# A hybrid decoder block on one core: outputs of the recurrence transposed by VectorE blocks and DMAs instead of TensorE

## The reference

```
def step(state, inp):
    q_n, k_n, u_n, w_n, qk_n, gc_n = inp
    v_new = u_n - einsum('bhcd,bhde->bhce', w_n, state)
    o = (einsum('bhcd,bhde->bhce', q_n * exp(gc_n)[..., None], state)
         + einsum('bhcs,bhse->bhce', qk_n, v_new))
    ...
    return state, o
...
o_a = o_a * rsqrt(mean(o_a * o_a, axis=-1, keepdims=True) + EPS)
o_a = o_a * gdn_norm_w * silu(gz)
y = sigmoid(mga) * (o_a @ w_branch_a) + sigmoid(mgb) * (o_b @ w_branch_b)
```

## Time and profile before

| | |
|---|---|
| median of 3 runs | 1130.29 us (1129.98 to 1130.35) |
| profiled execution | 1130.06 us |
| its span, first to last instruction | 1128.2 us |
| TensorE busy | 1118.4 us (99%) |
| ScalarE, VectorE, GpSimd busy | 456.5, 518.8, 538.7 us (40, 46, 48%) |
| recurrence, four chunks | about 163 to 400 us |

### The profile page before, as it was taken

How to read it: one execution, slowest core, us unless ns; L and a number is a source line. 1 busy time by engine, 2 the same in 40 slices (tenths; PEclk the granted TensorE clock), 3 DMA queues, 4 the chain that set the end, 5 groups by cost and what they waited for, 6 DMA issues and landing times.

```text
span 1128.2 us, 16308 instructions
## 1 busy us (share of the span) xinstructions
PE 1118.4 (99%) x5879; PEld 940.8 (83%) x5879; DVE 518.8 (46%) x1128; ACT 456.5 (40%) x759; POOL 538.7 (48%) x332
## 2 busy tenths in 40 slices
PE   9999999999999999999999999999999999999997
PEld 8788888888888888888888888888888888888885
DVE  5666456464646357777777562241222222220004
ACT  6465443435343365555555333423222222221122
POOL 5345674443524265555555544903444444444443
PEclk9999999999999999999999999999999999999999
DMA  7333333231313254444444375502333333222331
GB/s 212 80 91 95 101 105 103 66 103 57 94 48 112 71 155 118 123 123 128 122 120 121 105 246 147 188 26 75 93 93 93 96 106 95 93 94 94 100 105 75
DMA packets 169139, 120.45 MB, mean 107 GB/s; under 512 B 6665, under 2 KB 156274, under 8 KB 169090
## 3 DMA queue, kind: packets, MB, share of 16 engines
q1 hardware_dynamic: 156064, 98.73, 30.3%
q10 hardware_dynamic: 13026, 21.06, 6.0%
HBM read 111.35 MB, written 8.42 MB: 106 GB/s over the span
## 4 chain that ended last, share of the span: by engine, by line
PE 98%; DVE 0%; DMA 0%; ACT 0%; issue 0%; POOL 0%; POOLq 0%; DVEq 0%
PE ps L1684 66%; PE ps L2132 10%; PE ps L1798 7%; PE ps L1637 4%; PE ps L2052 4%; PE ps L2006 2%; PE ps L2106 1%; PE ps L1977 1%; PE ps L1976 1%; PE ps L1734 1%; PE ps L1746 0%; DMA x_nat<-in_x 0%; PE ps L1805 0%; PE ps L1757 0%; POOL rstd L575 0%
## 5 line engine op out<-in xcount | busy, mean ns | idle before, releaser
L580 POOL TENSOR_TENSOR w_lo<-raw,w_hi 128x1024 fp32r<-128x1024 f32 x159 | 384.0, 2415 | 477.6 <-ACT w_hi L749 477.6
L1684 PE MATMUL ps<-h_hi,w_hi 128*128 128x512 f32 x960 | 378.1, 394 | 0.0
L1684 PE MATMUL ps<-h_lo,w_hi 128*128 128x512 f32 x960 | 376.7, 392 | 0.0
L1684 PE MATMUL ps<-h_hi,w_lo 128*128 128x512 f32 x960 | 376.2, 392 | 0.0
L749 ACT ACTIVATE w_hi<-raw 128x1024 fp32r<-128x1024 f32 x159 | 168.6, 1060 | 440.5 <-PE ps L1684 339.3
L1684 PEld LDWEIGHTS ps<-h_hi,w_lo 128*128 128x128 f32 x960 | 180.4, 188 | 37.1 <-issue 0.4
L1684 PEld LDWEIGHTS ps<-h_hi,w_hi 128*128 128x128 f32 x960 | 180.4, 188 | 36.8 <-POOL w_lo L580 0.4
L1684 PEld LDWEIGHTS ps<-h_lo,w_hi 128*128 128x128 f32 x960 | 180.5, 188 | 35.7
L1591 DVE TENSOR_TENSOR f_lo<-tmp,f_hi 128x512 f32 (+1 forms) x22 | 41.7, 1895 | 143.6 <-ACT f_hi L1090 143.6
L1196 DVE SCALAR_TENSOR_TENSOR tmp<-ps,prm,tmp 128x511 f32<-128x511 f32 (+2 forms) x72 | 53.9, 748 | 46.6 <-ACT tmp L802 44.9
L1559 DVE TENSOR_TENSOR mixT<-ps,mixT 128x512 f32<-128x512 f32 x16 | 10.8, 687 | 124.4 <-PE ps L2132 107.5
(11 more groups left out here) (304 smaller groups left out, 1628.5 us busy)
## 6 DMA issues: line engine op xcount, KB each, us to landing
raw<-in_w_in SPq DMA_DIRECT2D x79, 512.0 KB, 3.9
raw<-in_w_gate SPq DMA_DIRECT2D x22, 512.0 KB, 3.7
raw<-in_w_up SPq DMA_DIRECT2D x22, 512.0 KB, 3.8
raw<-in_w_down SPq DMA_DIRECT2D x22, 512.0 KB, 3.4
gate_dram<-gate ACTq DMA_DIRECT2D x24, 256.0 KB, 2.0
cum<-cum_dram ACTq DMA_DIRECT2D x8, 512.0 KB, 7.3
raw<-in_w_branch_a SPq DMA_DIRECT2D x8, 512.0 KB, 4.2
raw<-in_w_branch_b SPq DMA_DIRECT2D x8, 512.0 KB, 4.1
```

The lines of the kernel that those rows point to most:

```text
L580: pool.tensor_tensor(w_lo[:, r % 2, :], raw[:, r, :], w_hi[:, r % 2, :], ALU.subtract)\
L1684: return pe.matmul(ps[:, bank, :], wts[wl][k], acts[xl][:, k, :], start=(n == 0), stop=(n == len(PASSES) - 1))
```

## The change

For the outputs of the first three chunks the eight turns on TensorE and the two copies on ScalarE are gone. Instead, in chunk c:

- VectorE, behind the Vb products, transposes ofn into o in one instruction of 128x1024, which transposes each 32x32 block in its place (o_blocks).
- ScalarE, behind `fill_done(n)` and ahead of the qkT copies, issues sixteen DMAs (`o_move`), one for each pair of 32-partition groups. Each moves 32 partitions x 8 heads x 32 elements (128 bytes in a piece) from o to its place in mixT (o_moved).
- ScalarE waits for all the moves so far (o_moved) before it writes o anew.
- VectorE waits for all the moves, and for the last chunk's copies, before it first reads mixT.

The last chunk's outputs are turned on TensorE as before. To keep the number of semaphores, most_turned is merged into x_turned, and out_done and down_done into half_done; each wait stands where it stood, with its count adapted.

```diff
+        MOVED = 16 * (P // LINE) ** 2
...
-            def o_out(c, bank=2):
-
-                for a in range(2):
-                    act.wait_ge(of_turned, led(of_turned, c * 2 + a + 1))
-                    act.activation(mixT[:, 4 * a:4 * a + 4, c * C:c * C + C], bank4(bank + a), ACT.Copy)\
-                        .then_inc(oT_ready, 1)
+            def o_out():
+
+                for a in range(2):
+                    act.wait_ge(of_turned, led(of_turned, a + 1))
+                    act.activation(mixT[:, 4 * a:4 * a + 4, T - C:T], bank4(a), ACT.Copy).then_inc(oT_ready, 1)
+
+            def o_move(c):
+
+                act.wait_ge(o_blocks, c + 1)
+                for b in range(0, P, LINE):
+                    for q in range(0, P, LINE):
+                        act.dma_start(mixT[q:q + LINE, :, c * C + b:c * C + b + LINE], o[b:b + LINE, :, q:q + LINE])\
+                            .then_inc(o_moved, 16)
...
             def chunk(c):
                 n = c * FILL + AHEAD
-                if c > 0:
-                    o_out(c - 1)
                 fill_done(n - 1)
                 fill_done(n)
+                if c > 0:
+                    o_move(c - 1)
                 for a in range(2):
                     act.wait_ge(qk_turned, c * 2 + a + 1)
                     act.activation(half(qkT, a), bank4(2 + a), ACT.Copy).then_inc(qkT_ready, 1)
...
+                if c > 0:
+                    act.wait_ge(o_moved, MOVED * c)
                 for h in range(H if c > 0 else 0):
                     act.wait_ge(qs_done, c * 2 - 2 + h // 4 + 1)
                     act.activation(o[:, h, :], bank4(4 + h // 4)[:, h % 4, :], ACT.Copy,
...
+                if c > 0:
+                    dve.wait_ge(of_ready, led(of_ready, c))
+                    dve.transpose(o[:, :, :].rearrange("p h c -> p (h c)"), ofn[:, :, :].rearrange("p h c -> p (h c)"))\
+                        .then_inc(o_blocks, 1)
                 dve.wait_ge(E_cut, c * 4 + 4)
                 dve.wait_ge(G_done, c * 2 + 2)
...
                 dve.wait_ge(zt_loaded, 16)
-                dve.wait_ge(oT_ready, led(oT_ready, 2 * TT))
+                dve.wait_ge(o_moved, MOVED * (TT - 1))
+                dve.wait_ge(oT_ready, led(oT_ready, 2))
...
-                if c > 0:
-                    o_turns(c - 1)
                 pe.wait_ge(E_exp, c + 1)
...
                 fill(FILLS[0])
-                pe.wait_ge(oT_ready, led(oT_ready, c * 2))
                 for a in range(2):
                     per_head(a, lambda h, n: mm(bank4(2 + a)[:, h, :], kT(n), kT(n)), G_done)
...
-                dve.wait_ge(down_done if n else out_done, 2 * t + a + 1)
+                dve.wait_ge(half_done, 2 * TT * n + 2 * t + a + 1)
...
-                    act.wait_ge(x_turned, k + 1)
+                    act.wait_ge(x_turned, k + 2)
```

More of the change, by code:

```diff
@@ L258, in hybrid_block @@
         x_scaled = sem("x_scaled")
-        most_turned = sem("most_turned")
         most_high = sem("most_high")
@@ L334, in hybrid_block @@
         oT_ready = sem("oT_ready")
+        o_blocks = sem("o_blocks")
+        o_moved = sem("o_moved")
         fill_taken = sem("fill_taken")
@@ L379, in hybrid_block @@
         wffn_loaded = sem("wffn_loaded")
-        out_done = sem("out_done")
+        half_done = sem("half_done")
         x2_added = sem("x2_added")
@@ L387, in hybrid_block @@
         wfin_loaded = sem("wfin_loaded")
-        down_done = sem("down_done")
         fin_ready = sem("fin_ready")
@@ L769, in _ @@
             most, rest = slice(0, (TT - 1) * P), slice((TT - 1) * P, T)
-            act.wait_ge(most_turned, 1)
+            act.wait_ge(x_turned, 1)
             act.wait_ge(prm_ready, 1)
@@ L775, in _ @@
             act.activation(w_hi[:, 0, 0:FIRST], raw[:, 0, 0:FIRST], ACT.Copy).then_inc(first_high, 1)
-            act.wait_ge(x_turned, 1)
+            act.wait_ge(x_turned, 2)
             act.activation(h_hi[:, 0, rest], ps[:, 0, rest], ACT.Copy, scale=prm[:, NMIX:NMIX + 1])\
@@ L993, in first_pair @@
                         .then_inc(q_taken, 1)
-                o_out(TT - 1, 0)
+                o_out()
                 high_ahead(FOX0, 2)
@@ L1664, in turn_rows @@
                 pe.wait_ge(x_scaled, 3)
-                scaled(2, 0).then_inc(most_turned, 1)
+                scaled(2, 0).then_inc(x_turned, 1)
                 for k in range(1, mid):
@@ L1941, in chunk, with o_turns @@
                 fill(((c + 1) * FILL + AHEAD) * len(PASSES) - at[0])
-            def o_turns(c, bank=2):
-                pe.wait_ge(of_ready, led(of_ready, c + 1))
+            def o_turns():
+                pe.wait_ge(of_ready, led(of_ready, TT))
                 for a in range(2):
                     for h in range(4):
-                        last = turn(bank4(bank + a)[:, h, :], ofn[:, 4 * a + h, :])
+                        last = turn(bank4(a)[:, h, :], ofn[:, 4 * a + h, :])
                     last.then_inc(of_turned, 1)
@@ L2026, in fox @@
                 else:
-                    unit(q, 2, hi, lo, [v_turn, lambda: o_turns(TT - 1, 0)], None, (4, 9))
+                    unit(q, 2, hi, lo, [v_turn, o_turns], None, (4, 9))
                     unit(q, 3, hi, lo)
@@ L2031, in _ @@
             fox(0, True, False)
-            pe.wait_ge(oT_ready, led(oT_ready, 2 * TT))
+            pe.wait_ge(oT_ready, led(oT_ready, 2))
             with pe.Fori(1, FH // 2) as i:
@@ L2086, in _ @@
                     last = out_product(0, n, k, 1, ends=True)
-                last.then_inc(out_done, 1)
+                last.then_inc(half_done, 1)
             for t in range(1, TT):
@@ L2153, in _ @@
                             last = down_product(k, t, n, p)
-                    last.then_inc(down_done, 1)
+                    last.then_inc(half_done, 1)
 _INS = ["x", "norm_mix_w", "w_in", "conv_w", "a_log", "dt_bias", "gdn_norm_w", "fox_f_bias", "w_branch_a",
```

## The result

The changed kernel takes 1158.08 us (median of 4 runs, 1155.65 to 1161.62), the kernel before 1130.13 (1129.87 to 1130.35). The ratio is 1.0251, with an interval of 1.0239 to 1.0263: 28.0 us or 2.5% slower. The direction was forecast, the size was not: 14.1 us were foreseen, and the time lies above the range.

The account below looks back on a forecast made before the run. TensorE, busy for 99% of the span, was taken as the bound. 1130.06 + 10.0 (holes less removed turns) + 3.9 (clock) = 1144.0 us, 1144.2 as a median; range 1134.0 to 1153.0.

Parts of the forecast that it names:

- The removed turns: TensorE at the head of chunks 1, 2 and 3: eight turns fewer, 0.87 us off each, 2.6 us in all.
- VectorE's transpose: Block transpose after the Vb products: 1.42 us, hidden in idle time ahead of Lq with 0.6 us to spare.
- The place of the price: Sixteen issues on ScalarE behind fill_done(n) delay qkT copies and Zm; TensorE waits 4.21 us for Zm in each chunk.
- the cost of an issue: ScalarE's time p per DMA issue: 0.52 us, lower end 0.40, taken from its own issues in a row.
- the rival of the full queue: 4096 pieces a chunk fill the queue: p = 0.81 us, hole 8.85 us, 1154.2 us; chance 0.12.
- the formula 16p - 4.11: Length in us of TensorE's wait for ScalarE's Zm in each chunk, p being the cost of an issue; 4.21 forecast.
- the clock: TensorE's clock falls to 1.2 GHz in most of the three holes: 1.3 us a chunk, 3.9 us in all.
- the row at the end of the span: Granted clock in the kernel before fell from 0.99 to 0.50 about 2.6 us after TensorE's last product.
- a bound of 2.58: Upper limit of the clock's price: stretch from Zm's turn to the next filling products, 2.58 us, at twice its duration.
- The clock that holds: Rival: TensorE's clock stays up in the holes, 1140.1 us, 1140.3 as a median; chance 0.29.
- The point of decision on the other side: At p = 0.31 us the hole equals the 0.87 us gained; below it the change is faster; chance 0.05.
- within 0.2%: Case of no measurable change, within 2.3 us, claimed for p between 0.30 and 0.32 us; chance 0.04.

Follow-up runs that it names:

- the kernel without moves: Changed kernel without the sixteen moves, block transposes kept, mixT of the first three chunks filled early with other data: 1127.45 us, ratio 0.9976.
- the one with SP: Changed kernel with each chunk's sixteen moves issued by SP between two weight loads, none by ScalarE: 1127.28 us, ratio 0.9975.
- ten moves: Changed kernel with ten of the sixteen moves, rest of mixT filled with other data: eight runs in two groups, median of all 1142.88 us.
- the kernel kept busy: Changed kernel with 26 extra products on TensorE ahead of its wait for Zm in chunks 1 to 3: 1146.91 us, ratio 1.0148.
- two idle stretches: Changed kernel with ten ScalarE moves ahead of fill_done(n) and six ahead of the last two Tm copies: 1127.79 us, ratio 0.9979.
- twelve moves: Changed kernel with twelve of the sixteen moves, a quarter of mixT filled with other data: 1152.97 us, ratio 1.019.

## Why the prediction was right or wrong, point by point

- **The removed turns**: right. 0.87 us a chunk; 2.7 us in all by the kernel without moves, 2.9 by the one with SP.
- **VectorE's transpose**: right in what it costs, nothing. It took 1.24 us where I had 1.42, and 0.92 us of the idle time ahead of Lq were left (chunk 1), where I had 0.6 (chunk 2).
- **The place of the price**: right. The sixteen issues behind fill_done(n), the idle time put down to issue, and TensorE's turns of Zm as the one waiting step, three times, all came as written.
- **The step that failed first: the cost of an issue.** I took 0.52 us, with 0.40 as a lower and no real upper end but the rival of the full queue, because the nearest rows had the same engine, the same dimensions and the same number of pieces. They had another source. It was 0.664, and sixteen times 0.14 make 2.3 us a chunk. With p = 0.664 the formula 16p - 4.11 gives 6.5; the hole was 6.05, as the stretch from the qkT copies to the end of Zm was 4.22 us (242.88 to 247.10) and not 4.60. Two short waits in it are gone for a ScalarE that comes late: the w_hi copy starts 0.97 us behind the first qkT copy, in rows 7 it was 1.19, and 0.42 us of idle time stand ahead of Zm instead of 0.58. The term came out at 17.9 - 2.6 = 15.3 us for a forecast of 10.0. The value 0.66 had no chance of its own, it only lay inside the range (p up to 0.7); an operand that differs from the row's is a reason to widen upward.
- **The step that failed most: the clock.** That it would fall was right, and the row at the end of the span was the right one to read, though its 2.6 us are no lower bound: with ten moves holes of 2.1 us were enough in five runs of eight. Its price was not. I took 1.3 us a chunk from a bound of 2.58, the stretch up to the next filling products. No row bore out that the clock comes back there. It stayed at 1.2 GHz for 8.2, 3.5 and 8.7 us of work in the three chunks. The cost is 11.2 / 3 = 3.7 us a chunk by the kernel kept busy and 12.7 / 3 = 4.2 by the holes, about three times my value and more than my bound.
- **Of the rivals** none was it. The full queue names a time near (1154.2) for the wrong reason: a quarter of the pieces left an issue at 0.62 us, and moves land 1.9 us after their issue (median). Its sum also has no clock in it, though a hole of 8.85 us was far beyond the 2.6 us at which I had the clock fall; with my own 3.9 us it would have been 1158.1, the measured time, by luck. The clock that holds has its own kernel, 1146.9. The point of decision on the other side, p = 0.31, was not tested; that the change gains when the issues don't reach Zm was, in the kernels without moves, with SP and with two idle stretches. By my own sum 2.3 us of difference are 0.05 us in p, so "within 0.2%" is p from 0.26 to 0.36 and not from 0.30 to 0.32.
- **The range** ended at 1153.0, which is p = 0.7 with the clock's term at its middle. Either error alone would have stayed inside: p = 0.664 with my clock term gives 1151.1, and my p with the measured clock term 1151.5 (11.2 us for the clock) to 1153.0 (12.7), the very end. Both came together, and the range had no place for that.
- **The Trainium skill** on issuing (DMA: Bandwidth & Descriptors, section "Issuing engines are not separate DMA queues") says that the time to start a DMA is usually small beside the DMA itself. Here one issue took 0.66 us and its DMA landed 1.9 us after it, and 0.66 us times sixteen in a row on an engine that is waited for was the largest part of the loss. The same sixteen on SP, or in two idle stretches of ScalarE, were free. Its warning on idle gaps (TensorE: Matmul & The Clock Gate, section "Why this matters for your kernels") agrees with the runs in its direction. But the gap from which it warns is longer than holes that did harm here: ten moves left holes of about 2 us, and five runs of eight were 8 to 11 us longer than the other three. The measurement decides.

## What to carry to other kernels

Price a DMA by the engine that issues it, times their number, and ask what stands behind them in that engine's order; a queue such as SP's that runs weight loads far ahead can take them for nothing. A hole in TensorE's stream costs its length and then, when it is long enough (here 0.7 us was not, 2 us at times, 3.4 us in every case seen), the clock: count both, for the second half of the time in which TensorE works at the lower clock, and do not assume that the clock is back with the next products. When a price is taken from a neighbouring row, name each operand in which the row differs, the memory that the source lies in too. And when two terms are uncertain, let the range hold both at their ends.

## What the runs showed of the hardware that I had not expected

- Issuing a DMA whose source is in SBUF holds ScalarE for 0.66 us, the same with a DRAM source for 0.50 us. Fewer pieces (618 ns against 632) or two dimensions instead of three (612) change little. On SP the median is 611 ns, with sixteen in 12.1 and 10.4 us; single issues took up to 1.8 us.
- A hole of about 2 us may or may not lower the granted clock, from one execution to the next; the times then stand in two groups, 1134 and 1142 to 1145 us. In kernels with longer holes the runs spread over 6 us where they otherwise spread over less than 1.
- With twelve moves, holes of 3.4 us cost more by the clock (1152.97 - 1137.7 = 15 us) than holes of 6 us with sixteen (11 to 13 us). The clock was down for about 37 us and 27 us in all, and TensorE had work in 35.5 and 20.4 us of them. What decides when it comes back stays open: behind twelve moves it was down for 13.5 us with TensorE busy for 13.35 of them.
- One block of Zm on VectorE took 2.41 us for a median of 0.27 while GpSimd made a w_lo beside it (eleven moves ahead of fill_done(n)). Why, these runs don't tell.
